# Feed-forward projections as seven block products, and the order of work at the borders of spatial gating

## The reference, cut to what matters

```python
def conv_glu_ffn(x, w_up, conv_w, conv_b, w_down):      # x: 512 x 1024, D_FF = 2816, CONV_WIDTH = 3
    h = x @ w_up
    a, b = h[..., :D_FF], h[..., D_FF:]
    ap = jnp.pad(a, ((0, 0), (CONV_WIDTH - 1, 0), (0, 0)))
    conv = conv_b + ap[:, 0:S] * conv_w[0]
    for j in range(1, CONV_WIDTH):
        conv = conv + ap[:, j:j + S] * conv_w[j]
    return (jax.nn.silu(conv) * b) @ w_down

def sgu_mixer(h, w_in, gain, w_s, b_s, w_out):           # 768 tokens in block 0, 512 in block 3
    u, v, z = jnp.split(h @ w_in, 3, axis=-1)
    u = jax.nn.gelu(u)
    v = rms_norm_2(jax.nn.gelu(v), gain)
    vc = v.reshape(bsz, length // SGU_CHUNK, SGU_CHUNK, SGU_GROUPS, SGU_GROUP_W)
    mixed = jnp.einsum('gpq,bcqgd->bcpgd', w_s, vc) + b_s.T[:, :, None]
    s = u * mixed.reshape(bsz, length, SGU_WIDTH)
    return (s * jax.nn.silu(z)) @ w_out
```

## Time and profile before

| | before |
|---|---|
| median of 3 runs | 4878.16 us (4870.84 to 4886.37) |
| the profiled execution | 4880.89 us, its span 4878.9 us |
| TensorE busy | 4649.4 us, 95% |
| VectorE, ScalarE, GpSimd busy | 1698.1, 1107.9, 682.4 us |
| mean granted TensorE clock | 0.976 of 2.4 GHz |
| the chain that ended last | 88% TensorE, 7% VectorE, 3% ScalarE |
| read from HBM | 334.46 MB |

### The profile page before, as it was taken

The page is one execution under the profiler, slowest core; times in us unless marked ns, Lnnn a source line. Parts: engine busy times, 40 slices in busy tenths (PEclk is TensorE's granted clock), DMA queues, the critical chain, the costliest instruction groups (busy, mean ns, idle before and its releaser), DMA issues.

```text
span 4878.9 us, 64908 instructions
## 1 busy us (share of the span) xinstructions
PE 4649.4 (95%) x27790; PEld 2775.4 (57%) x27790; DVE 1698.1 (35%) x3133; ACT 1107.9 (23%) x2166; POOL 682.4 (14%) x514
## 2 busy tenths in 40 slices
PE   8999999999999999999999988988999999999998
PEld 4444444444444458565555557777544555556887
DVE  3631110263211022224234338885310434421224
ACT  1131000113100021211133124443111333321220
POOL 1100000021000022334104200000000011003444
PEclk9989999998999999999999999999999999999999
DMA  3151212114222111111134422222211000011221
GB/s 125 51 217 61 78 70 71 69 61 174 94 78 75 65 59 69 52 61 50 71 127 133 132 87 79 78 76 87 88 51 58 25 19 29 19 61 69 87 84 64
DMA packets 115084, 378.49 MB, mean 78 GB/s; under 512 B 32752, under 2 KB 58480, under 8 KB 85360
## 3 DMA queue, kind: packets, MB, share of 16 engines
q1 hardware_dynamic: 103840, 332.92, 19.5%
q0 software_dynamic: 9808, 37.75, 2.3%
q10 hardware_dynamic: 1152, 3.67, 0.2%
HBM read 334.46 MB, written 39.85 MB: 77 GB/s over the span
## 4 chain that ended last, share of the span: by engine, by line
PE 88%; DVE 7%; ACT 3%; issue 2%; POOL 0%; DMA 0%; ACTq 0%; DVEq 0%; SPq 0%; POOLq 0%
PE ps L574 27%; PE ps L334 21%; PE ps L365 18%; PE ps L3753 2%; PE ps L2114 2%; PE ps L340 2%; PE ps L595 2%; PE ps L3675 1%; PE ps L1043 1%; PE ps L999 1%; PE ps L3764 1%; PE ps L3678 1%; PE ps L2769 1%; PE ps L3674 1%; PE ps L3676 1%
## 5 line engine op out<-in xcount | busy, mean ns | idle before, releaser
L574 PE MATMUL ps<-A,W 128*128 128x512 f32 (+1 forms) x3040 | 1317.4, 592 | 17.5 <-DVE A L544 8.8
L574 PEld LDWEIGHTS ps<-A,W 128*128 128x128 f32 x3040 | 580.3, 193 | 717.4 <-issue 702.0
L334 PE MATMUL ps<-A,W 64*64 64x64 f32 (+3 forms) x3264 | 660.4, 379 | 10.7 <-ACT A L3918 5.8
L334 PEld LDWEIGHTS ps<-A,W 128*128 128x128 f32 (+2 forms) x3264 | 348.5, 162 | 305.6 <-issue 282.0
L334 PEld LDWEIGHTS ps<-A 64*64 64x64 f32 (+2 forms) x8416 | 403.8, 148 | 144.6 <-issue 87.1
L334 PE MATMUL ps<-A 64*64 64x64 f32 (+3 forms) x8416 | 441.2, 238 | 42.2 <-ACT A L2985 14.0
L365 PE MATMUL ps<-A 128*128 128x256 f32 (+1 forms) x1632 | 438.2, 419 | 22.0 <-DVE A L453 18.7
L365 PE MATMUL ps<-A,W 128*128 128x384 f32 (+1 forms) x1536 | 432.3, 434 | 6.1 <-DVE A L1927 3.0
L365 PEld LDWEIGHTS ps<-A 128*128 128x128 f32 x1632 | 310.8, 191 | 129.7 <-DVE A L453 19.7
L365 PEld LDWEIGHTS ps<-A,W 128*128 128x128 f32 x1536 | 290.5, 190 | 127.5 <-issue 4.1
L486 ACT ACTIVATE A<-R 128x512 f32<-128x512 f32 (+1 forms) x96 | 51.7, 572 | 736.4 <-DVE R L1569 310.6
(11 more groups left out here) (398 smaller groups left out, 5124.0 us busy)
## 6 DMA issues: line engine op xcount, KB each, us to landing
W<-in_ada SPq DMA_DIRECT2D x48, 1024.0 KB, 5.0
W<-in_w_up SPq DMA_DIRECT2D x44, 1024.0 KB, 4.8
W<-in_w_down SPq DMA_DIRECT2D x32, 704.0 KB, 4.0
W<-in_w_in SPq DMA_DIRECT2D x18, 1024.0 KB, 4.8
W<-in_sgu_v SPq DMA_DIRECT2D x16, 1024.0 KB, 4.8
W<-in_sgu_u SPq DMA_DIRECT2D x16, 1024.0 KB, 4.8
W<-in_sgu_z SPq DMA_DIRECT2D x16, 1024.0 KB, 4.8
W<-in_sgu_o SPq DMA_DIRECT2D x16, 1024.0 KB, 4.7
```

The lines of the kernel that those rows point to most:

```text
L334: r = e.matmul(out, a, b, start=start and i == 0, stop=stop and i == len(pairs) - 1, skip_group_check=loose)
L574: t = e.matmul(ps, w[:, k, c:c + mc], x(k, seg), start=k == 0, stop=k == kt - 1)
```

## The change

**Feed-forward.** Each up slab is computed by seven products of 4 tiles by 256 tokens (the two 128-feature halves by the two token halves), each pair of down tiles by seven products of 11 tiles by 256 tokens. `ffn_pool` is new: GpSimd makes four sums per up slab (128x512) and per down pair (128x1408). VectorE gets the joins, the differences of h and of the gated tiles; the Silu is now in place. Down's weights come in a new layout of blocks; the loads of the even pairs go to the slots, those of the odd pairs into `A`, once the up projection is through. `weights_pool` waits for its blocks one by one.

**Gating.** At the start two products of v are begun in every block, and the differences of h move to places inside the v loop. The squares of v are made with every column group. For group 0, the first four products of both u and z run before anything else, and the first join of u comes before the scaling. The output products get banks of their own choice, and the first two pairs pause at their eighth tile.

The core of the diff:

```diff
-def seven_pe(pl, e, at, left, right, kt, n, ring, ready, kept_, slabs_):
+def seven_pe(pl, e, at, left, right, kt, n, ring, ready, kept_, slabs_, pause=None):
...
-    take(pl, a, ring)
+    take(pl, a, rings["A"])
     e.wait_ge(*free(pl, a))
-    into(a, 1, left.b11, right.b11, True).then_inc(*made.next((at, 1)))
+    if pause is not None:
+        into(a, 1, left.b11, right.b11, True, range(pause))
+        yield
+    into(a, 1, left.b11, right.b11, True, None if pause is None else range(pause, kt)).then_inc(*made.next((at, 1)))
...
-    for event in arrived:
+    for event in arrived[0]:
         e.wait_ge(*event)
     if before:
         e.wait_ge(*S_.seventh.at(before, 5))
     e.tensor_tensor(w.all_s1, w.all21, w.all22, ALU.add).then_inc(*made.next((at, 5)))
     if before:
         e.wait_ge(*S_.seventh.at(before, 6))
+    for event in arrived[1]:
+        e.wait_ge(*event)
     e.wait_ge(*made.at(at, 5))
     e.tensor_tensor(w.all_s2, w.all_s1, w.all11, ALU.subtract).then_inc(*made.next((at, 6)))
     e.tensor_tensor(w.all21, w.all11, w.all21, ALU.subtract).then_inc(*made.next((at, 7)))
     if before:
         e.wait_ge(*S_.seventh.at(before, 3))
+    for event in arrived[2]:
+        e.wait_ge(*event)
     e.wait_ge(*made.at(at, 6))
...
+def down_sp(pl, e, l):
+    S_, b, w = pl.S, pl.ffn, pl.ins["w_down"][l]
+    for p in range(4):
+        if p % 2 == 0:
+            for i, k in DOWN_ORDER:
+                slab_load(pl, e, ("w_down", l, p, i, k), w[p, i, k])
+            continue
+        if p == 1:
+            e.wait_ge(*S_.seventh.at(("up_b", l, 10), 4))
+            e.wait_ge(*S_.glu_done.at(l, 21))
+        for i, k in DOWN_ORDER:
+            if p == 3:
+                e.wait_ge(*S_.seventh.at(("down", l, 1), ((7, 3), (7, 4))[i][k]))
+            e.dma_start(b.odd[i][k], w[p, i, k].rearrange("p (k c) -> p k c", k=11)).then_inc(
+                *((S_.part0, S_.part1), (S_.part2, S_.part3))[i][k].next((l, p)))
...
+    names, ring = up_names(l), "01234567"
+
+    def products(at, first=False):
+        def ready(p, k):
+            if p == 1:
+                return [landed(pl, up_key(at))] * (k == 0) + [S_.normed.at(("n2", l), k, SC)] * first
+            if k:
+                return []
+            events = [S_.weights_summed.at(at, p)] if p in (5, 6, 7, 3) else []
+            if first and p in (5, 6, 7, 4):
+                events.append(S_.tokens_summed.at("h", l, p))
+            return events
+
+        return seven_pe(pl, e, at, up_blocks(pl, up_key(at)), b.x, 4, QUARTER, ring, ready, S_.first_kept.at(at),
+                        {4: [up_key(at)]})
+
+    begun = [products(at, True) for at in names[:2]]
+    for x in begun:
+        next(x)
+    for x in begun:
+        for _ in x:
+            pass
+    for at in names[2:]:
+        for _ in products(at):
...
+    def pair(p):
+        at = ("down", l, p)
+        key = lambda i, k: ("w_down", l, p, i, k)
+
+        def ready(q, k):
+            events = [down_landed(pl, l, p, *{1: (0, 0), 2: (0, 1), 4: (1, 1)}[q])] if k == 0 and q in (1, 2, 4) else []
+            if k == 0 and q in (5, 6, 7, 3):
+                events.append(S_.weights_summed.at(at, q))
+            if p == 0 and k == 10:
+                events.append(S_.glu_done.at(l, 20, 0) if q == 1 else S_.tokens_summed.at("g", l, 10, 4))
+            return events
+
+        released = {7: [key(0, 0), key(1, 0)], 3: [key(0, 1)], 4: [key(1, 1)]} if p % 2 == 0 else {}
+        return seven_pe(pl, e, at, down_blocks(pl, l, p), b.gx, 11, QUARTER, "0123456", ready, S_.joined.at(at, "x"),
+                        released)
+
+    for p in range(4):
+        for i, _ in enumerate(pair(p)):
+            if p and i in (1, 2):
+                sums_pe(pl, e, after, LATENT, 2 * p - 3 + i, LATENT[0])
...
+        at = ("up_a", l, i)
+        if i:
+            e.wait_ge(*S_.conv_done.at(l, 2 * i - 1))
+        kept_act(pl, e, at, QUARTER, b.a[:, 0, 2 + QUARTER:2 + S])
+        e.wait_ge(*S_.seventh.at(at, 2))
+        e.activation(b.a[:, 0, 2:2 + QUARTER], bank(pl, (at, "A"))[:, 0:QUARTER], ACT.Copy).then_inc(
+            *S_.act_projected.next(("up_a", l, i), frees=(at, "A")))
+        kept_act(pl, e, ("up_b", l, i), QUARTER, b.g[:, 2 * i, QUARTER:S])
+            y = b.cv[:, m % 2, :]
             e.wait_ge(*S_.conv_done.at(l, m))
-            if m >= 4:
-                e.wait_ge(*S_.glu_done.at(l, m - 4))
-            e.activation(b.bb[:, m % 4, :], b.cv[:, m % 2, :], ACT.Silu).then_inc(*S_.glu_act.next((l, m)))
+            e.activation(y, y, ACT.Silu).then_inc(*S_.glu_act.next((l, m)))
...
+    def differences(k, seg):
+        if k == 3:
+            e.wait_ge(*S_.normed.last())
+            e.tensor_tensor(t1, b12, b11, ALU.subtract).then_inc(*summed.next(("h", l, 5)))
+
+    normed_dve(pl, e, ("n2", l), LATENT, lambda k, seg: b.h[:, k, :], lambda k, seg: vec(pl, f"n2g{l}", k), differences)
+    e.wait_ge(*S_.normed.last())
+    e.wait_ge(*summed.at("h", l, 5))
+    e.tensor_tensor(t2, b22, t1, ALU.subtract).then_inc(*summed.next(("h", l, 6)))
+    e.tensor_tensor(b12, b22, b12, ALU.subtract).then_inc(*summed.next(("h", l, 7)))
+    e.wait_ge(*summed.at("h", l, 6))
+    e.tensor_tensor(t4, b21, t2, ALU.subtract).then_inc(*summed.next(("h", l, 4)))
...
+    for i in range(11):
...
+        c12, c21, c22 = b.a[:, 0, 2 + QUARTER:2 + S], b.a[:, 1, 2:2 + QUARTER], b.a[:, 1, 2 + QUARTER:2 + S]
+        for _ in joined_dve(pl, e, at, QUARTER, c12, c21, c12, c21, c22):
+            pass
+        even, odd = b.g[:, 2 * i, :], b.g[:, 2 * i + 1, :]
+        joining = joined_dve(pl, e, ("up_b", l, i), QUARTER, even[:, hi], odd[:, lo], even[:, hi], odd[:, lo],
+                             odd[:, hi])
+        e.wait_ge(*S_.act_projected.at("up_a", l, i))
+        e.wait_ge(*S_.joined.last())
+        if i == 0:
+            next(joining)
+        for m in (2 * i, 2 * i + 1):
+            y, x, w = b.cv[:, m % 2, :], b.a[:, m % 2, :], lambda j: vec(pl, f"cw{l}", 22 * j + m)
+            e.tensor_scalar(y, x[:, 2:2 + S], w(2), vec(pl, f"cb{l}", m), ALU.mult, ALU.add).then_inc(*wrote.next())
+            e.wait_ge(*wrote.last())
+            e.scalar_tensor_tensor(out=y, in0=x[:, 1:1 + S], scalar=w(1), in1=y, op0=ALU.mult, op1=ALU.add).then_inc(
+                *wrote.next())
+            e.wait_ge(*wrote.last())
+            e.scalar_tensor_tensor(out=y, in0=x[:, 0:S], scalar=w(0), in1=y, op0=ALU.mult, op1=ALU.add).then_inc(
+                *S_.conv_done.next((l, m)))
+        at = ("up_b", l, i)
+        y0, y1 = b.cv[:, 0, :], b.cv[:, 1, :]
+        if i:
+            next(joining)
+        e.wait_ge(*S_.glu_act.at(l, 2 * i))
+        e.wait_ge(*S_.seventh.at(at, 2))
+        e.tensor_tensor(even[:, lo], y0[:, lo], bank(pl, (at, "A"))[:, 0:QUARTER], ALU.mult).then_inc(
+            *S_.glu_done.next((l, 2 * i, 0), frees=(at, "A")))
+        next(joining)
+        e.wait_ge(*S_.joined.last())
+        e.wait_ge(*S_.glu_act.at(l, 2 * i + 1))
+        e.tensor_tensor(even[:, hi], even[:, hi], y0[:, hi], ALU.mult).then_inc(*S_.glu_done.next((l, 2 * i)))
+        e.tensor_tensor(odd, odd, y1, ALU.mult).then_inc(*S_.glu_done.next((l, 2 * i + 1)))
+        e.wait_ge(*S_.glu_done.last())
+        t1, t2, t4 = [t[:, i, :] for t in b.gt]
+        e.tensor_tensor(t1, even[:, hi], even[:, lo], ALU.subtract).then_inc(*summed.next(("g", l, i, 1)))
+        e.wait_ge(*summed.last())
+        e.tensor_tensor(t2, odd[:, hi], t1, ALU.subtract).then_inc(*summed.next(("g", l, i, 2)))
+        e.tensor_tensor(even[:, hi], odd[:, hi], even[:, hi], ALU.subtract).then_inc(*summed.next(("g", l, i, 3)))
+        e.wait_ge(*summed.at("g", l, i, 2))
+        e.tensor_tensor(t4, odd[:, lo], t2, ALU.subtract).then_inc(*summed.next(("g", l, i, 4)))
...
+        e.wait_ge(*S_.seventh.at(at, 1))
+        e.tensor_copy(x, a).then_inc(*made.next((at, "x")))
+        e.wait_ge(*made.last())
+        e.wait_ge(*S_.seventh.at(at, 6))
+        e.tensor_tensor(q, x, bank(pl, (at, "B"))[:, 0:QUARTER], ALU.add).then_inc(
+            *made.next((at, "q"), frees=(at, "B")))
+        e.wait_ge(*made.last())
+        e.tensor_tensor(v, q, c, ALU.add).then_inc(*made.next((at, "v")))
+        e.tensor_tensor(r0[:, hi], r0[:, hi], q, ALU.add).then_inc(*made.next())
+        e.tensor_tensor(r1[:, lo], r1[:, lo], q, ALU.add).then_inc(*made.next())
+        e.wait_ge(*made.at(at, "v"))
+        e.tensor_tensor(r1[:, hi], r1[:, hi], v, ALU.add).then_inc(*made.next())
...
+def ffn_pool(pl, e, l):
+    S_, b = pl.S, pl.ffn
+    for event in ends(pl, ("mix", l)):
+        e.wait_ge(*event)
+    e.memset(b.a[:, :, 0:2], 0.0).then_inc(*S_.pool_zeroed.next(("conv", l)))
+    before = None
+    for at in up_names(l):
+        weights_pool(pl, e, at, before, up_blocks(pl, up_key(at)), ([landed(pl, up_key(at))], [], []))
+        before = at
+    e.wait_ge(*S_.seventh.at(before, 4))
+    e.wait_ge(*S_.glu_done.at(l, 21))
+    before = None
```

(32 more changed lines are left out.)

194 lines of the change are left out of this document (104 added, 90 removed).

## The result

The kernel after the change takes 4750.5 us (median of four executions, 4747.9 to 4754.9) against 4878.5 of the kernel before on the same chip: a ratio of 0.9738, 95% interval 0.9724 to 0.9753. That is faster by 128 us. The forecast was 4748, range 4735 to 4776. The profiled execution took 4750.4 us, its span is 4748.5; that of before had 4878.9.

The account below looks back on a forecast made before the run. TensorE, busy 95% of the span, was taken as the bound. Feed-forward's 103.0 us and gating's 27.7 sum to 130.7; from 4880.9 that gives 4750.2, and 2.7 lower for the median, 4748, range 4735 to 4776.

Parts of the forecast that it names:

- The passes: Feed-forward on TensorE: finer 256-column passes save 35.9 us in up and 17.9 in down per layer, 107.6 for both layers.
- The 0.3 us that the start was to lose: Start of feed-forward: product 6 waits for VectorE's token differences, 0.3 us per layer, bounds 0 and 2.
- The cover in the up loop: Up loop: VectorE's joins and GpSimd's sums stay hidden beside TensorE, no stall; bounds 0 and 1.1 us per pair.
- the two equal convolution instructions: Up loop, VectorE: the convolution instructions that took 752 ns before would show a mean of 0.9 to 1.0 us.
- The first rival: Up loop: the join of up_b comes late through a third turn of GpSimd, 26 us, 4774 us; chance 0.12.
- two of each convolution's three: Up loop: only VectorE instructions with both operands in SBUF take turns with GpSimd, two of three per convolution.
- The slow rival: Up loop: every GpSimd sum blocks VectorE and reaches TensorE, 176 sums costing 223 us, 4971 us; chance 0.03.
- The up to down border: Between up and down: waits of 3.2 us replace 0.94, plus 2.3 us per layer; bounds plus 0 and plus 5.
- The fourth difference: Down's first pair: VectorE's last difference, in turns with GpSimd's sums, comes at 12.2, wanted at 9.7; 2.5 us lost.
- the sum's 0.65: Down's first pair: product 5, due at 4.75 us, starts at 5.4 after GpSimd's sum; 0.65 us lost.
- Gating: Gating blocks 0 and 3: removed waits and slow passes, mainly between v and u/z, gain 27.7 us, bounds 17 and 33.
- the eight products ahead: Gating, v to u/z: products 1, 5, 6, 7 of u and z give TensorE 20.6 us (block 0), 13.8 (block 3).

Follow-up runs that it names:

- e7_borders: Changed kernel with down's eleventh tile waiting only for the difference it reads, own banks for down's pairs, and gating's output sums reordered on GpSimd: 4729.6 us, ratio 0.9694.

## Why the prediction was right, and where its steps were off

**The passes.** 704 to 1232 and 352 to 616, each at the steady price of a 256-column pass: right. The forecast window of 268 to 270 us came out at 268.2. From the start of up to the start of down it was 305.2 us and is 268.6, minus 36.5. The 0.3 us that the start was to lose did not show.

**The cover in the up loop.** The forecast said v of up_b is there 0.6 to 1.8 us ahead of product 3; it is 2.1 us ahead, as in ten of eleven pairs a single sum of GpSimd falls beside the convolution, and none in the last. The mean of the two equal convolution instructions was forecast at 0.9 to 1.0 us and is 0.97 in the loop. The first rival (the join late, 4774) did not happen, but the margin is thin: what goes beyond 2.1 us of more work on VectorE reaches TensorE, as the runs with extra instructions and doubled sums show. That rival was also priced too high by its own terms: a third turn of 1.2 us against the 0.6 us left after two costs 0.6 a pair, 13 us and not 26. The step that was wrong is the sentence that, since joins from PSUM don't, only instructions with both operands in SBUF take turns, "two of each convolution's three". All three do (1108 ns for the tensor_scalar with doubled sums, 1433 for the extra ones, 10.96 us for the scaling); only those that read PSUM are spared. In the changed kernel it made next to no difference, because a sum fell beside the first instruction only once in each layer (0.76 in place of 0.55 us, in the first pair). The Trainium skill (SBUF — State Buffer, Who interferes with whom) lists tensor_scalar, in its two-port mode, among the instructions that can take the shared ports; these runs agree, and I had passed over that line.

**The slow rival** (every sum reaches TensorE, 4971) is refuted twice: leaving the sums out changes nothing, doubling them costs 22 us in the two stages and not 447.

**The up to down border.** Forecast were 3.2 us of waits in place of 0.94. The fourth difference came as foreseen (2.1 us, forecast 2.5), but the sum's 0.65 was not lost: product 1 had itself started 0.5 us late, waiting for a bank that the last join of up_b held, a wait that I had not seen. With other banks (e7_borders) that wait is gone and product 5 waits 0.40 us for the sum, as foreseen. The other half of the true cost, 1.95 us at a granted clock of 0.76 behind the wait, was missing too, although show such a stretch in gating, where I did count it. The first down pair took 37.4 us, where 36 to 37 were forecast. Down, from its first product to the next reciprocal, fell from 157.7 to 143.4 us, by 14.3, where 15.0 was forecast.

**Gating.** 15.0 and 12.0 us against 15.2 and 12.5. The removed wait and slow stretch between v and u came back in full. At the start of gating TensorE's waits for joins and GpSimd fell from 2.7 to 0.4 us in block 0 and by 1.5 in block 3 (2.1 and 1.3 forecast); no run undid these edits alone. The forecast took 0.4 us of gain at the output border of block 0 and nothing in block 3: the waits there went from 2.2 to 1.9 us and from 4.5 to 4.8. What the forecast did not see is that its three edits overlap: it named squares, join and the eight products ahead as one chain, and the join with either of the other two gives the 24 us.

**The total.** 130.7 forecast, 128.9 in the touched stages, 130.4 in the spans. The stages are the test of the forecast. That the median came within 3 us of 4748 is in part luck, as the untouched rest alone moves by up to 32 us from run to run. In feed-forward two small errors also had opposite signs: the start lost nothing, and the border lost more than forecast.

## What to carry to other kernels

When an engine gets new work beside a full one, price it by the slack at the first instruction that the bottleneck waits for, not by shares of busy time: here VectorE is busy half of the loop and had 2.1 us per 24. Let each consumer wait for the one result that it reads: naming the right difference instead of the last, with banks of their own for down, was worth 4 us per layer, with no work removed. And compare stages cut at fixed events; medians of the whole hide effects of 5 us that stages show to under 1.
